# Convolution borders on GpSimd, an earlier root on ScalarE, and two dense products moved in the head rounds of a two-layer hybrid block

## What is computed

```python
def _dn_inputs(p, dn_conv):                      # q, k, v of 8 heads, 128 wide
    y = silu(_dwconv(p[6], dn_conv))             # 3 taps along the tokens, zero padded
    q, k, v = split(y)
    return _l2norm(q), _l2norm(k), v, ...

def _gated_delta_chunked(q, k, v, g, beta, s0):  # in both directions, over chunks
    a_mat = where(strict, (kb @ k.T) * decay, 0)
    sol = triangular_solve(I + a_mat, [v * beta, kb * exp(gc)])
    ...                                          # scan over the chunks with state s

def _dn_output(o, gate, g):
    return _rmsnorm(o, g) * silu(gate)
```

## Time and profile before

| | |
|---|---|
| median of 3 runs | 2984.23 us (2984.11 to 2984.51) |
| the profiled execution, its own time | 2987.26 us |
| its span, first to last instruction | 2985.5 us |
| TensorE busy | 2935.2 us, 98% of the span |
| VectorE, ScalarE, GpSimd busy | 1930.0, 1460.4, 355.5 us |
| mean granted clock of TensorE | 0.998 of full |
| steady head round, layer 1 and layer 2 | 44.85 and 39.48 us |

### The profile page before, as it was taken

One profiled execution on the slowest core, in us unless ns is written; L12 is line 12 of the kernel. 1 busy time (PEld: TensorE's weight loads), 2 busy tenths in 40 slices (PEclk: granted clock), 3 DMA queues, 4 the chain that ended last, 5 costly groups with the idle time before them and its releaser, 6 DMA issues.

```text
span 2985.5 us, 50450 instructions
## 1 busy us (share of the span) xinstructions
PE 2935.2 (98%) x17768; PEld 2469.1 (83%) x17768; DVE 1930.0 (65%) x3479; ACT 1460.4 (49%) x2497; POOL 355.5 (12%) x272
## 2 busy tenths in 40 slices
PE   8999999999999999999999999999999999999998
PEld 5888888888887788888888888888888889799887
DVE  5766766766535834445665766757777766766777
ACT  5222258777546732234222242223788867644654
POOL 0000024434101000000000000000244321000000
PEclk9999999999999999999999999999999999999999
DMA  7544421211221032233444534434222114155454
GB/s 289 193 169 176 169 93 50 70 57 50 78 91 66 22 99 99 99 100 113 169 155 148 183 120 162 165 138 176 79 71 70 63 61 160 44 177 176 163 183 155
DMA packets 101845, 365.63 MB, mean 122 GB/s; under 512 B 11216, under 2 KB 12880, under 8 KB 101584
## 3 DMA queue, kind: packets, MB, share of 16 engines
q1 hardware_dynamic: 98384, 353.02, 34.3%
q10 hardware_dynamic: 3328, 10.81, 1.1%
HBM read 362.67 MB, written 1.11 MB: 122 GB/s over the span
## 4 chain that ended last, share of the span: by engine, by line
PE 90%; ACT 4%; DVE 3%; issue 2%; DMA 1%; SPq 0%; DVEq 0%; ACTq 0%; POOLq 0%; POOL 0%
PE bank L2125 69%; PE bank L2104 4%; PE bank L2106 2%; PE bank L2683 1%; PE bank L2398 1%; PE bank L2423 1%; PE bank L2465 1%; PE bank L2656 1%; PE bank L2669 1%; PE bank L2395 1%; PE bank L2455 1%; PE bank L2476 1%; ACT ada_raw L946 1%; PE bank L2488 1%; PE bank L2486 1%
## 5 line engine op out<-in xcount | busy, mean ns | idle before, releaser
L584 ACT ACTIVATE whi<-raw 128x1024 fp32r<-128x1024 f32 x518 | 546.7, 1058 | 991.4 <-PE bank L2125 964.1
L2125 PE MATMUL bank<-uh,whi 128*128 128x512 f32 (+1 forms) x2688 | 1000.9, 372 | 6.2 <-DVE ul L1395 2.0
L2125 PE MATMUL bank<-uh,wlo 128*128 128x512 f32 (+1 forms) x2688 | 980.3, 365 | 0.0
L2125 PE MATMUL bank<-ul,whi 128*128 128x512 f32 (+1 forms) x2688 | 974.8, 363 | 0.0
L1312 DVE TENSOR_TENSOR wlo<-raw,whi 128x1024 fp32r<-128x1024 f32 x476 | 583.4, 1226 | 368.7 <-ACT whi L584 353.4
L2125 PEld LDWEIGHTS bank<-uh,whi 128*128 128x128 f32 x2688 | 508.3, 189 | 95.8 <-issue 23.0
L2125 PEld LDWEIGHTS bank<-uh,wlo 128*128 128x128 f32 x2688 | 508.3, 189 | 73.0 <-issue 3.4
L2125 PEld LDWEIGHTS bank<-ul,whi 128*128 128x128 f32 x2688 | 508.6, 189 | 71.2 <-issue 3.8
L2125 PE MATMUL bank<-bh,whi 128*128 128x512 f32 (+1 forms) x930 | 340.1, 366 | 0.8 <-DVE bl L2044 0.8
L2125 PE MATMUL bank<-bl,whi 128*128 128x512 f32 (+1 forms) x930 | 337.6, 363 | 0.0
L2125 PE MATMUL bank<-bh,wlo 128*128 128x512 f32 (+1 forms) x930 | 337.6, 363 | 0.0
(11 more groups left out here) (309 smaller groups left out, 3838.6 us busy)
## 6 DMA issues: line engine op xcount, KB each, us to landing
raw<-stream SPq DMA_DIRECT2D x520, 512.0 KB, 3.3
ada_raw<-stream SPq DMA_DIRECT2D x132, 512.0 KB, 4.3
gc_row<-gc_rows ACTq DMA_DIRECT2D x16, 512.0 KB, 3.7
m<-stream SPq DMA_DIRECT2D x5, 512.0 KB, 12.1
h<-h_in SPq DMA_DIRECT2D x1, 2048.0 KB, 9.8
cst<-consts SPq DMA_DIRECT2D x1, 1104.0 KB, 9.2
lmat<-stream SPq DMA_DIRECT2D x2, 512.0 KB, 11.5
gc_row<-stream SPq DMA_DIRECT2D x2, 512.0 KB, 12.0
```

The costliest lines, as they stand in the source:

```text
L584: act.activation(whi[:, j, :], raw[:, j, :], ACT.Copy).then_inc(hi_ready, 1)
L2125: last = mm(bank[j if to is None else to][:, c0:c1], w(t, a), x[:, t, c0:c1], start=n == 0, stop=n == 3 * kts - 1)
```

## The change

Four things are changed, all in the head rounds.

1. The tap on ScalarE is one instruction for all columns, with the bias of the inner ones. A new step on GpSimd, `edges`, subtracts from the first and the last column of each sequence what is too much there, in place. VectorE's first half of the convolution waits for it (`edge_ready`). Two subtractions in `head_vectors` go.
2. The inverse root of the output stands ahead of ScalarE's copies of v and k, and VectorE's scaling by it stands between the two first levels and not ahead of both.
3. The first half of v's convolution stands one mask later, and its second half between the two instructions that follow the last level.
4. In the second layer the stretch after the product of k and q has three dense products and no longer five, and the scan has one more behind each of its first two steps.

```diff
+                def edges(b, n):
+                    j = (1, 0, 2)[n]
+                    a = c0 // CTX if j == 0 else 0
+                    x = kraw[:, :] if j == 1 else qkv[:, j, :]
+                    ends = x.rearrange("p (s t) -> p s t", s=2)[:, a:2, 0:256:255]
+                    bias = hx[:, j:j + 7:6].rearrange("p (s e) -> p s e", s=1).broadcast_to([128, 2 - a, 2])
+                    pool.wait_ge(E["tap_ready"], 3 * (l * DNH + b) + n + 1)
+                    pool.tensor_tensor(ends, ends, bias, ALU.subtract).then_inc(E["edge_ready"], 1)
...
                     if after:
                         split(P[("head", l)][0] + b + 2, 0)
                     if follow:
+                        edges(b + 1, 0)
+                        edges(b + 1, 1)
                         masked(o + 1)
                         if not after:
                             split(P[("head", l)][0] + b + 2, 0)
-                        for n in range(2):
-                            low_squares(b + 1, n)
+                        low_squares(b + 1, 0)
+                        edges(b + 1, 2)
+                        low_squares(b + 1, 1)
...
-                for lo, hi, e in ((1, CTX - 1, 9), (0, 1, 0), (CTX - 1, CTX, 6)):
-                    last = act.activation(y[:, :, lo:hi], p[:, :, lo:hi], ACT.Identity, scale=hv[:, 5 + 3 * j:6 + 3 * j],
-                                          bias=hx[:, e + j:e + j + 1])
-                last.then_inc(E["tap_ready"], 1)
+                act.activation(y, p, ACT.Identity, scale=hv[:, 5 + 3 * j:6 + 3 * j], bias=hx[:, 9 + j:10 + j]).then_inc(E["tap_ready"], 1)
...
                     act.activation(eo[:, 0, c0:T], bank[6][:, c0:T], ACT.Square).then_inc(E["osq_ready"], 1)
+                    act.wait_ge(E["on_sum"], o + 1)
+                    rsqrt(eo[:, 1, c0:T], bank[7][:, c0:T], 128, E["on_rstd"])
...
-                if output:
-                    act.wait_ge(E["on_sum"], o + 1)
-                    rsqrt(eo[:, 1, c0:T], bank[7][:, c0:T], 128, E["on_rstd"])
...
-                    dve.wait_ge(E["tap_ready"], 3 * o + n + 1)
+                    dve.wait_ge(E["edge_ready"], 3 * o + n + 1)
...
+                    first_level(0)
                 if output:
                     dve.wait_ge(E["on_rstd"], o + 1)
...
-                    first_level(0)
                     first_level(1)
...
-                        if follow and at in (3, 7, 10):
+                        if follow and at in (3, 7, 11):
...
-                        if follow and at in (5, 9, 11):
-                            prep_conv(l, b, at // 4 - 1 if at < 11 else 2, first=False)
+                        if follow and at in (5, 9):
+                            prep_conv(l, b, at // 4 - 1, first=False)
...
-                fill = ((4, 5, 6) if c0 else (4, 6, 6)) if output else (8, 10, 6)
+                fill = ((4, 3, 6) if c0 else (4, 6, 6)) if output else (8, 10, 6)
...
-                    ahead, amid, behind, rest = (0, 3, 3, 3), (2, 2, 2, 2), (1, 1, 0, 1) if c0 else (1, 0, 0, 1), 3
+                    ahead, amid, behind, rest = (0, 3, 3, 3), (2, 2, 2, 2), (2, 2, 0, 1) if c0 else (1, 0, 0, 1), 3
```

More of the change, by code:

```diff
@@ L284, in build @@
         E = {n: sem(n) for n in (
-            "hv_ready", "hb_ready", "hgc_ready", "tap_ready", "conv_ready", "silu_ready", "hsq_ready", "low_square",
+            "hv_ready", "hb_ready", "hgc_ready", "tap_ready", "edge_ready", "conv_ready", "silu_ready", "hsq_ready", "low_square",
             "l2_sum", "l2_rstd", "kn_ready", "qn_ready", "k_turned", "v_turned", "ktok_ready", "vtok_ready",
@@ L540, in step @@
                             split(P[("head", l)][0] + b + 2, 0)
-                        for n in range(2):
-                            low_squares(b + 1, n)
+                        low_squares(b + 1, 0)
+                        edges(b + 1, 2)
+                        low_squares(b + 1, 1)
                         split(P[("head", l)][0] + b + 2, 1)
                         split(P[("head", l)][0] + b + 2, 2)
+                for n in range(3):
+                    edges(0, n)
                 masked(l * DNH)
@@ L917, in output_and_front @@
                     act.activation(ktok, bank[5][:, :], ACT.Copy).then_inc(E["ktok_ready"], 1)
-                if output:
-                    act.wait_ge(E["on_sum"], o + 1)
-                    rsqrt(eo[:, 1, c0:T], bank[7][:, c0:T], 128, E["on_rstd"])
-                if front:
                     act.wait_ge(E["kq_sum"], f + 1)
@@ L1662, in head_vectors @@
                 steps.sync()
-                dve.tensor_tensor(e[0], e[3], e[0], ALU.subtract)
-                steps.do(dve.tensor_tensor(e[2], e[3], e[2], ALU.subtract))
-                steps.sync()
             def prep_vec(l, b):
@@ L1779, in head @@
                     dve.tensor_tensor(c4d(XT[:, d, :]), bc(ident, TC, 128), c4d(bank[4 + d][:, :]), ALU.subtract).then_inc(E["xt_ready"], 1)
+                    if follow and d == 0:
+                        prep_conv(l, b, 2, first=False)
                     if not follow and d == 0:
```

## The result

The changed kernel takes 3035.23 us, the median of 4 runs (3032.68 to 3037.48); the kernel before, beside it, took 2984.37 us (2984.11 to 2985.99, 4 runs). The ratio is 1.0166, with a 95% interval of 1.0153 to 1.0179: 51 us slower, where 3031 us and a range of 3010 to 3046 had been forecast. The profiled execution took 3037.48 us itself, with a span of 3035.6 us and a mean granted clock of 0.990.

A forecast was written before the change was run, and what follows sets the result against it. TensorE, busy 2935.2 of 2985.5 us, was taken as the bound. Waits less gains and first rounds (28.8 + 6 + 2 = 36.8) plus clock (6.6 + 3.9) made 47.3 us on 2984.23: 3031 us, range 3010 to 3046.

The forecast's parts named there:

- waits less gains, layer 1, six rounds: Level 3 late behind GpSimd's border, less 0.4 us from level 6: +4.8 us a round, 28.8 us.
- waits less gains, layer 2, six rounds: Level 3 late behind GpSimd's border, less 1.0 and 0.4 us of gains: +1.0 us a round, 6 us.
- first rounds: Each layer's first round: third border behind GpSimd's late squares, 1 us a layer (bounds 0 and 1.5), 2 us.
- clock, layer 1: TensorE's clock falls after the wait in each of six rounds, 1.1 us each: 6.6 us.
- clock, layer 2: TensorE's clock falls in half of the six rounds, at 1.3 us: 3.9 us.
- everything costs more: Rival: border instruction 0.61 us, clock falling in every second-layer round, longer slow stretch in the first: 3043 us; chance 0.06.
- Level 6 in the first layer: TensorE's wait at level 6 gone through shorter third tap and moved third convolution: 0.4 us a round gained.
- The scan's 0.4: Second layer: two dense products moved to the scan fill its waits, 0.4 us a round gained.
- the 1.0 for levels 5 and 6: Second layer: waits of level 6 (0.4 + 0.5) and small ones of level 5 gone, some 1.0 us a round.
- The clock holds: Rival: waits come as said, but TensorE's products between them keep the upper clock level: 3021 us; chance 0.22.
- The wait is shorter: Rival: 4.0 us net in the first layer, 0.3 in the second, clock holds: 3010 us; chance 0.05.
- The faster case: Rival: borders ready when VectorE comes to them, only gains left, 13 to 15 us: 2970 us; chance 0.05.

The follow-up runs named there:

- the second experiment: The kernel before with the borders on GpSimd alone, in the change's place in GpSimd's order: 3043.49 us, ratio 1.0192.
- the third: The changed kernel with k's and q's borders ahead of GpSimd's split, still behind the other products: 3001.66 us, ratio 1.0049.
- the fourth: The changed kernel with k's border behind q's products with the decays, q's ahead of the split, v's ahead of the low squares: 2980.25 us, ratio 0.9977.
- the fifth experiment: The changed kernel with unread products added ahead of level 3 in six rounds a layer (16 first layer, 6 second): 3022.87 us, ratio 1.0123.
- the eighth: The first experiment's kernel with both halves of the third convolution back where they were before the change: 2983.72 us, ratio 0.9995.
- the first experiment: The changed kernel without the borders on GpSimd, ScalarE's tap again three instructions: 2979.18 us, ratio 0.9978.
- tenth experiment: The sixth's kernel with the inverse root back behind ScalarE's copies of v and k: 2981.17 us, ratio 0.9982.
- sixth: The first experiment's kernel with VectorE's scaling by the root back ahead of both first levels: 2977.10 us, ratio 0.9971.
- the ninth experiment: The fourth's kernel with the sixth's scaling and v's border between the two instructions of k's low squares: 2975.46 us, ratio 0.9968.

## Why the prediction was right

**The mechanism** was right: the second experiment has all of the loss, the third takes the split out of it one for one, the fourth all of it. GpSimd's chain was forecast at 8.62 and 5.87 us and took 8.51 and 5.81; the border instruction takes 0.20 us (forecast 0.25, lower bound 0.17). on_ready came 0.16 us later in the first layer (forecast 0.2) and 0.27 earlier in the second (0.1). Level 3 was 4.75 and, in its second direction (558.66), 5.0 us late where 5.0 and 5.2 were forecast; in the second layer 1.85, not 2.1.

**The sum**, each term against what the fifth experiment lets one separate:

| | forecast | measured |
|---|---|---|
| waits less gains, layer 1, six rounds | 28.8 | 27.1 |
| waits less gains, layer 2, six rounds | 6 | 6.2 |
| first rounds | 2 | 3.6, about 1.3 of it the clock |
| clock, layer 1 | 6.6 | 12.2 |
| clock, layer 2 | 3.9 | 4.0 |

(27.1 is 296.2 - 269.1, 6.2 is 243.0 - 236.8, 3.6 is 0.7 + 2.9.) The median lies 4 us above the forecast, and one term is most to blame: the clock in the first layer was mis-sized by 5.6 us. The other differences are smaller, and some go the other way (1.7 us less of waiting in the first layer, and 1.6 us less from the slow stretch outside the rounds that went). The forecast took a single slow stretch of 3.4 us for each of the six rounds, after the one example in the profile before; six there were, but each of 6.83 us (556.50 to 563.30 above). The rival in which everything costs more had named a longer slow stretch. In the second layer three of the six rounds had one, as forecast, at some 1.3 us each (4.0 / 3).

**The gains.** Level 6 in the first layer: forecast 0.4, measured 0.41. The reason was half wrong: the shorter tap was named beside the third convolution, and the eighth and fourth experiments show that the convolution does it alone. The tap was also mis-sized, by taking it from the row of a SiLU: its one instruction takes 0.78 us, not 0.63, so it is 0.48 us shorter than the 1.26 of before and not some 0.6. In the changed kernel, second layer:

```profile
2363.32 0.78 ACT L826 ACTIVATE scr<-bank,hv 128x512 f32<-128x512 f32 x1
```

In the second layer 1.4 was forecast for level 5, level 6 and the scan; the changed kernel has 2.1 - 1.0 = 1.1 of it (its second direction of level 3 is 2.1 us late, its rounds with the clock held 1.0 us longer), which is the 0.77 of the first experiment and the 0.35 of the shorter tap. The scan's 0.4 is about confirmed (0.36). What failed is the 1.0 for levels 5 and 6: the convolution brings 0.5 and the shorter tap 0.35. Each of these prices was taken with the other parts in place, and they are not a sum.

**A wait that the forecast did not see.** It gave the root's wait as gone with nothing in its place, and costed the scaling's new place by GpSimd's start alone. Behind the first level of the first direction TensorE waits for l_ready, and the scaling now stands ahead of that on VectorE. The root does pay (0.38 a round, tenth experiment), the scaling's place takes back 0.16 (sixth). That the forecast's net of 1.0 us a round is what was measured is luck: two of its errors, gains and a delay that were both 0.3 too high, cancel.

**The first rounds.** The place was right (the third border behind late squares), the size was not: 2.9 us in the second layer above an upper bound of 1.5. GpSimd's timeline of the changed kernel there:

```profile
2191.40 2.53 POOL L499 TENSOR_TENSOR m<-gc_row,cst 128x512 f32<-128x512 f32 x2 [2.43 <-DMA gc_row<-gc_rows]
2193.88 2.38 POOL L491 TENSOR_TENSOR wlo<-raw,whi 128x1024 fp32r<-128x1024 f32 x1
2196.22 1.03 POOL L517 TENSOR_TENSOR scr<-kraw 128x512 f32<-128x512 f32 x1
2197.34 1.28 POOL L520 TENSOR_TENSOR bl<-scr,bh 128x512 fp32r<-128x512 f32 x1
2198.58 0.20 POOL L510 TENSOR_TENSOR scr<-scr,hv 128x4 f32<-128x4 f32 x1
```

In a layer's first step the split stands behind the masked decays, not ahead of them, and its 2.38 us were left out of the estimate. VectorE's third convolution then waits 2.62 us. TensorE has 1.60 us of waits from it, and behind them a slow stretch of 3.41 us, at 2201.72, for which no term of the forecast stood:

```profile
2198.67 0.50 PE L2513 MATMUL bank<-bl,onesr 128*128 128x512 f32 x1 [0.56 <-POOL bl L520]
2200.21 3.13 PE L2432 MATMUL bank<-scr_r,lmat 128*128 128x128 f32 x16 [1.04 <-DVE scr_r L1786]
```

The rest of the round from there, first in the changed kernel, then in the fifth, which has the same two waits (0.68 and 1.04) and no slow stretch behind them:

```profile
2200.21:2218.57 18.36, 18.26 (x117) 16.32 (x118) 9.62 (x26) 13.38 (x29) 4.78 (x2) 0.91 0.10 29
2190.74:2207.79 17.05, 16.95 (x117) 15.00 (x118) 9.61 (x25) 13.26 (x29) 4.78 (x2) 1.00 0.10 32
```

So about 1.3 of the 2.9 us are the clock again. Without them the round is 1.6 us late, just above the bound.

**The rivals.** "The clock holds" falls with the profile. "The wait is shorter" wanted 4.0 us net and no fall; it was 27.1 / 6 = 4.5, with the falls. "Everything costs more" wanted 0.61 us for a border instruction, which took 0.20. The faster case named the right switch, the border ahead of the split and the products, and gave 2970 us for it, some 14 less than before; the fourth experiment, which throws it, gives 2980, 6.0 less than the kernel beside it, mostly because the gains counted for it in the second layer, 1.4 to 1.8 a round, came to 0.78 (39.48 - 38.70).

## What to carry to other kernels

When a small instruction is moved to an idle engine, cost its place in that engine's order and not its length: 0.20 us of work cost 57 us because 8.5 us (5.8 in the second layer) stood ahead of it in each round, and it was free in a gap where the engine waited for itself. When TensorE is full, a saving on another engine is worth only what it takes from a wait, and where the next wait on the path stands right behind, it must be taken together with it (the fourth against the ninth experiment). Cost a wait of TensorE with the clock behind it, and see whether work can be put into the wait.

## What the runs showed of the hardware

Ahead of level 3 the fall of the clock grows with the wait. A wait of 4.6 us brought a slow stretch of 6.83 us in each of six rounds; in the second experiment one of 4.4 us brought 6.83 in four of six, 3.41 in the other two; one of 2.3 us (third experiment) a stretch of 3.41 us in three of six; one of 2.0 us (second layer) one of 3.41 us in three of six in the changed kernel and in two of six in the second experiment; those of 1.1 and 0.7 us behind added products brought none in twelve.

But the length of a wait does not decide it alone. In the first round of the second layer the second experiment's TensorE waited 3.41 us ahead of level 6, and the granted clock stayed at 1.00:

```profile
2201.41 0.29 PE L2404 MATMUL bank<-ada_raw 128*128 128x64 f16 x4 [3.41 <-DVE ada_raw L1780]
```

In that round two shorter waits, of 0.56 and 1.04 us, had a slow stretch behind them in the changed kernel, and 0.68 and 1.04 had none in the fifth. And in the kernel before the slow stretch at 424.7 has no wait ahead of it: from 421.20 to 424.70 TensorE is shown busy for the whole 3.50 us, from 421.90 to 424.50 with products of 8 and 16 columns. What decides between such cases is open.

The Trainium skill ("TensorE: Matmul & The Clock Gate", section "Why this matters for your kernels") says that an idle gap between bursts returns TensorE to half rate; the falls at level 3 agree, and come at gaps of 2.0 and 2.3 us, shorter than that section warns of, while the longer gap of 3.41 us without a fall does not agree.

That TensorE needs only to be kept busy, with products nobody reads, was worth 12 us of the median, and 16 us of the rounds: the fifth kernel's profile has two single slow stretches more outside them.

GpSimd's instruction on 4 elements a partition takes 0.20 to 0.21 us, and neighbours overlap: the second starts 0.15 us behind the first (556.36 to 556.51).
